# Entry projections of the prompt tokens as three one-pass products of split operands, with the loads, the band products and a normalisation rearranged

## What is computed

```python
h = layer_norm(x, P['ln0_g'], P['ln0_b'])           # entry, 1056 tokens x 1024
z = h @ P['w_in'][l]                                # 1024 -> 2568 columns
qa, ka, va, ub, vb, xc, qkv, zg, bd, ad = jnp.split(z, idx, axis=-1)
vn = layer_norm(jax.nn.gelu(v).reshape(b, t, G_B, DG_B), ln_g, ln_b)     # v is vb
win = cs[:, POOL_BUF + 1:..., ch] - cs[:, POOL_BUF + 1 - w:..., ch]      # windows of 2, 4, 8, 16 tokens over xc
```

## Time and profile before

| | |
|---|---|
| runs, us | 1586.08, 1592.48, 1593.78 (median 1592.48) |
| profiled execution | 1597.02 us, span 1595.2 us, mean granted clock 0.928 |
| PE busy | 1381.3 us (87% of the span), weight loads 963.9 us |
| DVE, ACT, POOL busy | 645.6, 550.7, 159.7 us |

### The profile page before, as it was taken

One profiled execution on the slowest core, in us unless ns is written; L12 is line 12 of the kernel. 1 busy time (PEld: TensorE's weight loads), 2 busy tenths in 40 slices (PEclk: granted clock), 3 DMA queues, 4 the chain that ended last, 5 costly groups with the idle time before them and its releaser, 6 DMA issues. The chain is left out here.

```text
span 1595.2 us, 25519 instructions
## 1 busy us (share of the span) xinstructions
PE 1381.3 (87%) x9942; PEld 963.9 (60%) x9943; DVE 645.6 (40%) x1025; ACT 550.7 (35%) x1072; POOL 159.7 (10%) x154
## 2 busy tenths in 40 slices
PE   4998999689999889888997997989982799998980
PEld 2444999665567777776886996767862333332320
DVE  4331555248732223445773002328546233322226
ACT  1222323258752633434212213423220333342425
POOL 0000000003320132210000000000000122321210
PEclk9999999879999878999998998999985899999995
DMA  9111121114004310003104106515243588897336
GB/s 331 44 56 40 30 61 40 49 56 159 1 20 142 102 47 16 3 3 122 60 40 145 40 16 226 227 60 197 85 165 152 210 265 265 269 299 231 77 60 227
DMA packets 83684, 185.03 MB, mean 116 GB/s; under 512 B 12948, under 2 KB 48923, under 8 KB 77171
## 3 DMA queue, kind: packets, MB, share of 16 engines
q1 hardware_dynamic: 76523, 157.14, 27.5%
q0 software_dynamic: 6912, 25.17, 6.7%
q10 hardware_dynamic: 144, 1.25, 0.2%
HBM read 144.31 MB, written 39.31 MB: 115 GB/s over the span
## 5 line engine op out<-in xcount | busy, mean ns | idle before, releaser
L3104 PE MATMUL bank<-arena,hT 128*64 x384 | 178.3, 608 | 9.9 <-DVE hT L3220 5.6
L3104 PEld LDWEIGHTS bank<-arena,hT 128*64 128x64 f32 x384 | 51.5, 140 | 112.2 <-issue 109.4
L479 PE MATMUL bank<-arena,hT 128*128 128x512 f32 x256 | 112.6, 598 | 0.0
L2176 PE MATMUL bank<-hT_rest,f_w_high 128*128 128x352 f32 x288 | 93.2, 324 | 0.0
L3107 PE MATMUL bank<-arena,hT 128*64 128x512 f32 x192 | 91.3, 621 | 0.0
L3130 PE MATMUL bank<-arena,hT 128*64 x192 | 87.5, 598 | 0.7 <-ACT hT L3171 0.7
L3107 PE MATMUL bank<-h,hT 128*64 128x512 f32 x192 | 87.0, 596 | 0.0
L479 PEld LDWEIGHTS bank<-arena,hT 128*128 128x128 f32 x256 | 48.6, 193 | 58.3 <-issue 58.2
L3060 POOL DMA_INDIRECT expert_sums<-hT,row_slot x24 | 48.2, 2010 | 222.4 <-DVE hT L3226 161.4
L2175 PE MATMUL bank<-hT_high,q_w_high 128*128 128x352 f32 x192 | 62.7, 326 | 4.0 <-DVE q_w_low L2468 4.0
L2175 PE MATMUL bank<-f_h_high_a,f_w_high 128*128 128x352 f32 x180 | 59.0, 328 | 6.7 <-DVE f_w_low L689 6.7
(11 more groups left out here) (501 smaller groups left out, 3163.9 us busy)
## 6 DMA issues: line engine op xcount, KB each, us to landing
arena<-in_ex_wg_dram SPq DMA_DIRECT2D x16, 1024.0 KB, 5.0
arena<-in_ex_wu_dram SPq DMA_DIRECT2D x16, 1024.0 KB, 8.4
arena<-in_ex_wd_dram SPq DMA_DIRECT2D x16, 1024.0 KB, 12.1
tokens<-h SPq DMA_DIRECT2D x24, 512.0 KB, 2.6
arena<-in_cache_mem_k_dram SPq DMA_DIRECT2D x8, 1024.0 KB, 4.9
arena<-in_w_in_dram SPq DMA_DIRECT2D x12, 512.0 KB, 4.0
h<-tokens SPq DMA_DIRECT2D x6, 1024.0 KB, 7.6
h<-in_x_prompt_dram SPq DMA_DIRECT2D x8, 512.0 KB, 8.8
```

The source lines that it names most:

```text
L479: last = nc.tensor.matmul(ps[bank][0:r, 0:n], hT[:, k, i * P:i * P + r], wt[:, k, col:col + n], start=(k == 0), stop=(k == KC - 1))
L2176: nc.tensor.matmul(out, high, w_low, start=False, stop=False)
L3104: nc.tensor.matmul(ps[UPB[u % 2]][rows_of(0), :], xT[:, u % 2, k, rows_of(0)], gate_up_of[:, bass.ds(slot, 1), :, k, :].rearrange("p a g f ...
```

## The change

1. Entry: tokens and weights of kv and vx are split into high (float32r) and rest. Each prompt tile's 16 float32 matmuls become 48 one-pass ones: for kv and for vx 8 high by high, 8 rest by high, 8 high by rest. ACT's copy of the turned tile becomes three casts to the high part; DVE subtracts for the rest, in three pieces. ACT rounds the weights in five pieces per half, DVE makes the rests.
2. The turn of tile i+1 moves between vx's first and second group of 8.
3. The sample tile's float32 matmuls take high and rest of the weights in turn (64 instead of 32), on an unrounded copy of its turned tokens (`keep_raw`); `bd|ad` take high and rest of the tokens (48 instead of 24).
4. Features uses entry's split tokens: `round_h` and `low_h` go there.
5. Loads: three slots hold the token tiles, and tile i+3 is loaded after tile i is stored and turned. kv weights come before tile 1, vx before tile 2; of the constants only the identity comes first. The first two weight blocks of features are loaded after the sample tile's evacuation, into space that a part of the rounded weights has held.
6. Features: ACT's inverse deviation for the gate's norm moves from its end to behind block 2, and DVE's three passes ahead of the last block's rest.
7. Gate and pool: `bandprev` takes 16 columns instead of 128.

```diff
@@ SP, entry
-            for i in range(TILES):
-                sp.dma_start(h[0:rows(i), i, :], x_tile(T, i)).then_inc(x_in[min(i // 2, 2)], 16)
...
+            load(0)
+            sp.dma_start(g, row_bc(T['ln0_g'])).then_inc(ln_in, 16)
+            sp.dma_start(b, row_bc(T['ln0_b'])).then_inc(ln_in, 16)
+            sp.dma_start(wt[:, :, kv_cols], w_view[:, :, KA:KA + 512]).then_inc(w_kv, 16)
+            load(1)
+            sp.dma_start(wt[:, :, vx_cols], w_view[:, :, VB:VB + 512]).then_inc(w_vx, 16)
+            load(2)
+            sp.dma_start(wt[:, :, 1024:1032], w_view[:, :, BD:BD + 8]).then_inc(w_ba, 16)
+            sp.dma_start(c.const[:, P:], T['const_tables'][:, P:]).then_inc(const_in, 16)
             for i in range(TILES):
                 sp.wait_ge(normed, i + 1)
+                sp.dma_start(c.tokens_dram[i * P:i * P + rows(i), :], x(i)).then_inc(h_out, 16)
+                if i + SLOTS < TILES:
+                    sp.wait_ge(turned, 2 * i + 2)
+                    sp.wait_ge(h_out, 16 * (i + 1))
+                    load(i + SLOTS)
@@ DVE, entry
+            def low_h(i):
+                for n, (q, ks) in enumerate(PARTS):
+                    dve.wait_ge(hh_ok, 3 * i + (1, 3, 3)[n])
...
+                    nc.vector.tensor_tensor(h_low[:, ks[0]:ks[-1] + 1, tok(i)], src, h_high(ks, tok(i)).bitcast(F32),
+                                            ALU.subtract).then_inc(hl_ok, 1)
+            normalise(0)
+            low_w(kv_cols, wh_kv, wl_kv)
+            low_h(0)
+            normalise(1)
+            low_w(vx_cols, wh_vx, wl_vx)
+            for i in range(1, TILES):
...
+                low_h(i)
+                if i + 1 < TILES:
+                    normalise(i + 1)
@@ ACT, entry
             deviation(0)
+            round_w(kv_cols, w_kv, wh_kv)
+            round_h(0)
+            deviation(1)
+            round_w(vx_cols, w_vx, wh_vx)
+            for i in range(TILES + 1):
+                if i + 1 < TILES:
+                    round_h(i + 1)
+                if i < TILES:
+                    evac_kv(i)
+                if i + 2 < TILES:
+                    deviation(i + 2)
+                if i < NT:
+                    evac_vx(i)
+                if i >= 1:
+                    evac_kT(i - 1)
@@ PE, entry
+                one_pass(kv, i, kv_cols, "high_high")
+                pe.wait_ge(hl_ok, 3 * i + 3)
+                one_pass(kv, i, kv_cols, "low_high")
+                if i == 0:
+                    pe.wait_ge(wl_kv, len(SPLIT))
+                one_pass(kv, i, kv_cols, "high_low").then_inc(proj_kv, 1)
...
+                one_pass(vx, i, vx_cols, "high_high")
+                turn(i + 1)
+                one_pass(vx, i, vx_cols, "low_high")
...
+                one_pass(vx, i, vx_cols, "high_low").then_inc(proj_vx, 1)
@@ ACT, features
-            round_h(0)
             round_w(0)
-            round_h(1)
-            round_h(2)
             round_w(1)
...
+                if n == 2:
+                    nc.scalar.preload_act_table_set(EXPLN)
+                    act.wait_ge(stats, 1)
+                    link(nc.scalar.activation(mom[:, 1, :], mom[:, 1, :], ACT.Ln, bias=c.eps, scale=1.0 / DH))
+                    nc.scalar.activation(mom[:, 1, :], mom[:, 1, :], ACT.Exp, scale=-0.5).then_inc(rstd_ok, 1)
@@ PE, gate and pool
-                        last = nc.tensor.matmul(out, xc[:, i - 1, g * DH:(g + 1) * DH], band(f"bandprev{g}"),
-                                                start=False, stop=True)
+                        last = nc.tensor.matmul(out[:, 0:POOLB + 1], xc[:, i - 1, g * DH:(g + 1) * DH],
+                                                band(f"bandprev{g}", P, POOLB + 1), start=False, stop=True)
```

More of the change, by code:

```diff
@@ L304, in stage_entry @@
     c.place(start=c.free_at, wtok=KC * 1056)
-    c.place(start=at, ring=2 * KC * P, lng=D, lnb=D, ktok=2 * 256)
+    c.place(start=at, ring=2 * KC * P, lng=D, lnb=D, ktok=2 * 256, hTh=KA_ * TOK)
     c.f_w_in = [c.sem(f"f_w{n}") for n in range(2)]
@@ L460, in turn, with one_pass @@
                     last.then_inc(turned, 1)
+            def one_pass(out, i, cols, which):
+                for k in range(KC):
+                    weights = w_low[:, k, cols] if which == "high_low" else high(k)[:, cols]
+                    tokens = h_low[:, k, tok(i)] if which == "low_high" else h_high(k, tok(i))
+                    last = nc.tensor.matmul(out, tokens, weights, start=(which == "high_high" and k == 0),
+                                            stop=(which == PASSES[-1] and k == KC - 1))
+                return last
@@ L500, in _ @@
                     turn_k(i - 1)
+            pe.wait_ge(w_ba, 16)
             pe.wait_ge(pad_ok, 1)
+            pe.wait_ge(const_in, 16)
+            pe.wait_ge(hl_ok, 3 * TILES)
             for n in range(GRP):
-                for k in range(KC):
+                t = slice(n * GT, (n + 1) * GT)
+                for k, first in [(4 * m + j, part == 0) for m in range(2) for part in range(2) for j in range(4)]:
                     q = k % 4 * NS
-                    last = nc.tensor.matmul(ps[(0, 1, 4)[n]][q:q + NS, 0:GT], wt[:, k, 1024:1056], hT[:, k, n * GT:(n + 1) * GT],
-                                            start=(k < 4), stop=(k >= 4))
+                    tokens = h_high(k, t) if first else h_low[:, k, t]
+                    last = nc.tensor.matmul(ps[(0, 1, 4)[n]][q:q + NS, 0:GT], wt[:, k, 1024:1056], tokens.bitcast(F32),
+                                            start=(k < 4 and first), stop=(k >= 4 and not first))
                 last.then_inc(baT_mm, 1)
@@ L729, in _ @@
                 ins.then_inc(conv_ok, 1)
-            for n in range(10, len(plan)):
-                low_w(n)
+            low_w(10)
             dve.wait_ge(rstd_ok, 1)
@@ L737, in _ @@
                                     ALU.add).then_inc(normed, 1)
+            low_w(11)
 def stage_gate_and_pool(c):
```

178 lines of the change are left out of this document (101 added, 77 removed).

## The result

| | before | after |
|---|---|---|
| median of the runs, us | 1593.13 (1586.08 to 1597.2) | 1553.15 (1549.19 to 1554.62) |
| profiled execution, its span | 1597.02, 1595.2 | 1554.62, 1552.8 |
| mean granted clock | 0.928 | 0.934 |
| PE, weight loads, DVE, ACT busy | 1381.3, 963.9, 645.6, 550.7 | 1358.2, 987.7, 656.8, 552.5 |

What follows compares the result with a forecast made beforehand. PE was taken to bound entry. Terms 20.0 + 8.6 - 7.4 + 3.5 + 11.3 + 1.7 = 37.7 us, from the median 1592.48, gave 1554.8, stated as 1555; range 1545 to 1569.

Steps and rivals of the forecast that it cites:

- PE paces entry and the step decides: Entry, tiles 1 to 7: PE sets the pace; one-pass products stepping by 0.226 us win 20.0 us.
- chain: Entry, from one turn to the next: casts, rest and normalisation take 8.3 us, against 11.85 on PE.
- A tile becomes 48 x 0.226 + 0.97: Entry, one prompt tile: 48 one-pass products plus two turns, given as 11.85 us instead of 14.71.
- Weight loads in line: Rival, entry: each product waits for its own weight load, step 0.414, 72 us more, total 1627; chance 0.03.
- The array's rate: Rival, entry: products step by 0.2145 to 0.216 us instead of 0.226, total 1551; chance 0.07.
- The start: Start of entry: earlier loads let tile 0 end at 32.3 instead of 40.92, 8.6 us won.
- The sample tile, `bd` and `ad`: End of entry: the sample tile's and `bd|ad` products double on PE's path, 7.4 us lost.
- Start and end of features: Features: fewer casts and rests at its start win 3.5 us; the norm's passes moved from its end win 11.3.
- I leave the half-clock start as it is: Start of features: a 2.5 us gap remains, so no gain or loss is counted for the half-clock start.
- Gate and pool: Gate and pool, the bands: eight records per tile become narrow, 1.7 us won over seven tiles.
- What is won before it should reach the end whole.: Stages behind gate and pool: unchanged, starting when it ends, so the whole 37.7 us should reach the total.

Runs made afterwards that it cites:

- the variant with filled idle time: Kernel after with bands loaded during features and unread identity transposes where PE would wait in features and gate and pool; 1553.8 us, ratio 0.9735.

## Why the prediction was right, and where only its total was

- **PE paces entry and the step decides.** Right. 20.00 of 20 busy, no wait in the tile, chain 8.2 against 8.3. The term was mis-sized: 17.4 instead of 20.0. "A tile becomes 48 x 0.226 + 0.97" is 11.82, not the 11.85 written, and measured are 12.22: the step of 0.231 costs 0.24 per tile, and the extra time behind each of the two turns 0.16 together. The second could have been read from the output projection of the kernel before, where the first product behind a turn also stands 0.31 ahead of the next.
- **Weight loads in line.** Out. The loads of entry take 188 to 189 ns and products step by 0.231, less than the two together, so they lie beside each other. The Trainium skill (TensorE: Matmul & The Clock Gate, Part 3, What overlaps and what doesn't) wants a different row group for that; here all use the whole array, and the measurement decides.
- **The array's rate.** Out too: the step is 0.231, further from 0.2145 to 0.216 than the 0.226 that the prediction took. The same page of the Trainium skill (Back-to-back issue gap) gives about 216 ns for an isolated product of 512 columns and about 131 ns for a stream of products with their loads; the trace shows 231 and speaks against both.
- **The start.** 7.8 instead of 8.6. PE's first product came at 18.24 where I had 17.6, and it ran below full clock for 6.6 us (18.24 to 24.87), not only for the first eight products. The wait for the vx weights, which I had at 1 to 2 us, didn't come: kv ended at 26.71, when those weights had been rounded (26.1).
- **The sample tile, `bd` and `ad`.** 6.9 instead of 7.4: the products doubled, as said.
- **Start and end of features.** 3.7 where I had 3.5, and 11.3 to the tenth; the latter is shown by taking it back and by doing it alone. The products in between lost 0.8, which I had at nothing ("I leave the half-clock start as it is"): in the 10 us from the first product on the granted clock is 0.76 after, where it was 0.85.
- **Gate and pool.** 0.3 instead of 1.7. The price of the narrow product was right, but the wait for the bands grew from 0.73 to 2.59 and the half clock behind it reached into a second tile, which took it back. I had read the price of a tile at full clock, and the first tiles aren't; and the wait for the load was no term of the sum.
- **"What is won before it should reach the end whole."** This sentence failed. The changed part is 32.8 us shorter, not 37.7, and the unchanged stages are 9.6 shorter in the profile, where the granted clock makes the difference, and 5 to 7 by the medians. The total came out right by luck: the one offset the other. In the variant with filled idle time the same effect went the other way and ate 7 us.

## What to carry to other kernels

Price a product by its step between starts in the nearest place with the same shapes, and add what its neighbours cost: the first product behind a turn took 0.08 more, and after a gap PE ran for 6 us below full clock. Before a gain of less than 10 us in a kernel of this length is credited to an edit, compare the unchanged stages of the two profiles one by one; here they moved by 7 to 10 us with the granted clock, for the change in the kernel after and against it in one of its variants. When a chain is to be covered by another engine, take the cover away in a run: its own period (8.16 us here) says how much room is left.

## What was not expected of the hardware

- Two unchanged stages come out at different lengths, delta 186 to 189 or 193 to 194 us, cross 282.2 to 282.7, 285.5 to 285.8 or 288.6 to 288.7, with the same work, and the granted clock accounts for the difference (in one stretch 0.54 against 0.91). In these runs the lengths follow neither how early a stage starts nor how much work lies ahead of it.
- Products of the same shape step by 0.231 in entry, in either order of them, and by 0.226 in the output projection.
- At the start of entry, 18.24 to 24.87, products took 0.45, then 0.38 on average, before they came to 0.23, although PE had made its first turn from 11.53 on (1.94 us, against 1.04 in later tiles) and the window from 10 to 20 us shows a granted clock of 1.00. The trace's clock records begin only at 24.4 us, where the products come to 0.23, so ahead of that the products, not that column, tell the rate.
